# Sums of squares for a retention head: two of four feature tiles added on VectorE, and all weight roundings of the stage on VectorE

## The reference, cut to what matters

```
def retention(xn, w_in, w_out):
    proj = xn @ w_in
    q, k, v, g = split(proj)                 # 1024, 1024, 2048, 2048 columns
    ...
    out = inner + cross                      # per head: decayed (q k^T) v
    out = rms_norm(out).reshape(B, S, H * dv)      # over the 512 features of a head
    return (silu(g) * out) @ w_out

def rms_norm(x):
    return x * rsqrt(mean(x * x, axis=-1) + EPS)
```

## Time and profile before

| | |
|---|---|
| Median of 3 runs | 1396.87 us (1387.72, 1396.87, 1397.72) |
| Profiled execution | 1386.03 us, of which the span from first to last instruction is 1384.2 us |
| TensorE busy, granted clock | 97% of the span, 0.988 |
| VectorE, ScalarE, GpSimd busy | 67%, 50%, 10% |
| Gate slots and heads, output projection | 744 to 802.6 us, 802.6 to 850 us of the span |

### The profile page before, as it was taken

How to read it: one execution, slowest core, us unless ns; L and a number is a source line. 1 busy time by engine, 2 the same in 40 slices (tenths; PEclk the granted TensorE clock), 3 DMA queues, 4 the chain that set the end, 5 groups by cost and what they waited for, 6 DMA issues and landing times.

```text
span 1384.2 us, 24555 instructions
## 1 busy us (share of the span) xinstructions
PE 1342.2 (97%) x9631; PEld 1243.7 (90%) x9631; DVE 924.5 (67%) x1197; ACT 691.9 (50%) x959; POOL 142.6 (10%) x116
## 2 busy tenths in 40 slices
PE   8998999999999999999999999999999979999997
PEld 8997988999988999888999978999888967899986
DVE  6876753677556777447744476877657684799964
ACT  5664344532334544345344565666546374666652
POOL 0000151000000000000000330222200000025410
PEclk9999999999999999999999999999999988999999
DMA  7552322310045555554553354555554521455562
GB/s 278 183 172 84 125 107 92 128 57 31 0 177 184 183 186 182 182 183 164 186 192 133 117 178 172 183 182 182 198 212 153 183 92 57 170 185 182 182 216 103
DMA packets 30314, 213.03 MB, mean 154 GB/s; under 512 B 3488, under 2 KB 3616, under 8 KB 5152
## 3 DMA queue, kind: packets, MB, share of 16 engines
q1 hardware_dynamic: 29088, 206.72, 42.8%
q0 software_dynamic: 1152, 5.24, 1.2%
HBM read 210.90 MB, written 1.05 MB: 153 GB/s over the span
## 4 chain that ended last, share of the span: by engine, by line
PE 88%; DVE 6%; ACT 4%; DMA 1%; issue 1%; SPq 0%; DVEq 0%; ACTq 0%
PE lin L522 54%; PE lin L591 20%; PE aux L2199 2%; PE aux L2213 1%; PE aux L2211 1%; ACT whi L496 1%; PE aux L2343 1%; PE aux L2089 1%; DMA raw<-in_stream 1%; PE aux L2456 1%; PE aux L2359 1%; DVE ht L1288 1%; DVE ro L1809 1%; PE aux L2161 1%; ACT xhi L746 0%
## 5 line engine op out<-in xcount | busy, mean ns | idle before, releaser
L503 DVE TENSOR_TENSOR wlo<-raw,whi 128x2048 fp32r<-128x2048 f32 x182 | 423.2, 2328 | 181.1 <-ACT whi L496 180.7
L522 PE MATMUL lin<-xhi,whi 128*128 128x256 f32 (+1 forms) x1776 | 508.1, 286 | 2.3 <-DVE xlo L1299 1.8
L522 PE MATMUL lin<-xlo,whi 128*128 128x256 f32 (+1 forms) x1776 | 502.7, 283 | 0.0
L522 PE MATMUL lin<-xhi,wlo 128*128 128x256 f32 (+1 forms) x1776 | 500.0, 282 | 0.0
L496 ACT CAST whi<-raw 128x2048 fp32r<-128x2048 f32 x193 | 366.9, 1903 | 216.0 <-DMA raw<-in_stream 183.5
L522 PEld LDWEIGHTS lin<-xhi,whi 128*128 128x128 f32 x1776 | 334.7, 188 | 5.3 <-issue 4.0
L522 PEld LDWEIGHTS lin<-xhi,wlo 128*128 128x128 f32 x1776 | 336.8, 190 | 0.0
L522 PEld LDWEIGHTS lin<-xlo,whi 128*128 128x128 f32 x1776 | 335.4, 189 | 0.4
L689 POOL TENSOR_TENSOR wlo<-raw,whi 128x2048 fp32r<-128x2048 f32 x11 | 51.2, 4652 | 519.0 <-ACT whi L496 335.9
L1897 DVE SCALAR_TENSOR_TENSOR ft<-fy,par,ft 128x254 f32<-128x254 f32 (+1 forms) x176 | 91.0, 557 | 5.9 <-DVE ft L1897 0.2
L591 PE MATMUL lin<-wlo,fhi 128*128 128x512 f32 x176 | 69.6, 396 | 0.0
(11 more groups left out here) (411 smaller groups left out, 2102.7 us busy)
## 6 DMA issues: line engine op xcount, KB each, us to landing
raw<-in_stream SPq DMA_DIRECT2D x193, 1024.0 KB, 4.9
gp<-in_gains POOLq DMA_DIRECT2D x6, 512.0 KB, 3.9
c<-in_const SPq DMA_DIRECT2D x1, 1652.0 KB, 17.5
h<-in_x SPq DMA_DIRECT2D x2, 544.0 KB, 4.0
c<-in_const POOLq DMA_DIRECT2D x1, 1024.0 KB, 5.1
ht<-in_xtok POOLq DMA_DIRECT2D x1, 1024.0 KB, 6.9
out<-ht SPq DMA_DIRECT2D x1, 512.0 KB, 2.6
out<-ht SPq DMA_DIRECT2D x2, 256.0 KB, 2.2
```

Source lines behind the costliest of these rows:

```text
L503: nc.vector.tensor_tensor(wlo[:, s0 % 4], raw[:, s0 % 4], whi[:, s0 % 4].bitcast(F32), ALU.subtract).then_inc(lo_ready, 1)
L522: ins = nc.tensor.matmul(out, a, b, start=start and n == 0, stop=stop and n == 2)
```

## The change

Three edits. (1) A new step `pairs` hh on VectorE stands ahead of `squares` hh in the written order. It adds the second half of the squares (tiles 2 and 3) to the first (tiles 0 and 1), one instruction of 128x512. (2) `squares` waits for that addition and multiplies two tiles by the ones in place of four: eight ones-products in the stage, not sixteen. (3) GpSimd makes no rounding in this stage; VectorE makes the rounding of slot j + 3 behind the eviction of every gate j, and no longer waits for GpSimd ahead of the output projection.

```diff
 RETENTION = [..., ("gate", 3), ("hi", 3), ("silu", 3),
-             ("squares", 0), ("root", 0), ("product", 2), ("readout", 2), ("gate", 4), ("hi", 4), ("finish", 0),
-             ("squares", 1), ("root", 1), ("product", 3), ("readout", 3), ("high", 0), ("gate", 5), ("hi", 5),
-             ("low", 0), ("finish", 1), ("squares", 2), ("silu", 4), ("silu", 5), ("high", 1), ("gate", 6), ("hi", 6),
-             ("low", 1), ("root", 2), ("squares", 3), ("finish", 2), ("gate", 7), ("hi", 7), ("root", 3), ("silu", 6),
+             ("pairs", 0), ("squares", 0), ("root", 0), ("product", 2), ("readout", 2), ("gate", 4), ("hi", 4), ("finish", 0),
+             ("pairs", 1), ("squares", 1), ("root", 1), ("product", 3), ("readout", 3), ("high", 0), ("gate", 5), ("hi", 5),
+             ("low", 0), ("finish", 1), ("pairs", 2), ("squares", 2), ("silu", 4), ("silu", 5), ("high", 1), ("gate", 6), ("hi", 6),
+             ("low", 1), ("root", 2), ("pairs", 3), ("squares", 3), ("finish", 2), ("gate", 7), ("hi", 7), ("root", 3), ("silu", 6),
              ("silu", 7), ("high", 2), ("finish", 3), ("low", 2), ("high", 3), ("low", 3)]
 # GpSimd
-            pool_low(pool, FIRST["rg"] + 6, FIRST["ro"] + 3)
 # VectorE
             def gate(j):
...
-                if j < 3:
-                    load_lo(s + 3, 0)
+                load_lo(s + 3, 0)
+
+            def pairs(hh):
+                after(dve, f"ro{hh}_0")
+                after(dve, f"ro{hh}_1")
+                q = rsq[:, hh % 2]
+                nc.vector.tensor_tensor(q[:, 0:2], q[:, 0:2], q[:, 2:4], ALU.add).then_inc(S("ro_pairs"), 1)
...
-            dve.wait_ge(lo_ready, FIRST["ro"] + 3)
 # TensorE
             def squares(hh):
-                after(pe, f"ro{hh}_0")
-                after(pe, f"ro{hh}_1")
+                pe.wait_ge(S("ro_pairs"), hh + 1)
                 b = fill(f"rn{hh}")
-                for e in range(4):
-                    ins = nc.tensor.matmul(b[:, 0:SEQ], ones[:], rsq[:, hh % 2, e], start=e == 0, stop=e == 3)
+                for e in range(2):
+                    ins = nc.tensor.matmul(b[:, 0:SEQ], ones[:], rsq[:, hh % 2, e], start=e == 0, stop=e == 1)
```

More of the change, by code:

```diff
@@ L1815, in low @@
                     .then_inc(S("rlo"), 1)
-            todo = {"gate": gate, "finish": finish, "low": low}
+            todo = {"gate": gate, "pairs": pairs, "finish": finish, "low": low}
             for name, n in RETENTION:
```

## The result

| | before | after |
|---|---|---|
| Median | 1396.57 us (4 runs, 1387.72 to 1397.72) | 1423.78 us (4 runs, 1409.95 to 1425.06) |
| Ratio | | 1.0224, 95% interval 1.0162 to 1.0285 |
| Profiled execution, span | 1386.03, 1384.2 us | 1425.0, 1423.2 us |
| Granted clock, mean | 0.988 | 0.969 |

A forecast was written before the change was run, and what follows sets the result against it. TensorE was taken to bound the stage, with one 2.46 us hole at its end. Waits of 26.5 us less 3.5 and 2.5, plus 8.0 for the clock, gave 28.5 on 1396.87: 1425 us, range 1405 to 1434.

The forecast's parts named there:

- the turns: TensorE and VectorE wait for each other around the ones-products; net of products and hole, 20.5 us slower.
- the clock: Half-speed stretches after the four waits: 2.4 us for heads 1 to 3, 0.8 for head 0; 8.0 us slower.
- The place at which TensorE waits: Ones-products of heads 0 to 3 wait for additions queued on VectorE behind each gate slot's end; 26.5 us in all.
- What is removed: Half the ones-products (3.46 us) and the stretching of VectorE by GpSimd roundings (hole, 2.46 us): gains of 5.9 us.
- The hole at the third output slot: TensorE's 2.46 us wait at 816.39 in the output projection, for a late low part; forecast to close.
- Rival (a): Additions of heads 0 to 3 are hidden and relief of VectorE counts: 5.9 us faster, 1391; chance 0.08.
- Rival (b): Clock doesn't fall, or one short stretch follows each wait: 20.5 to 27.3 us slower; some 0.25 of the 0.85.
- Rival (c): Clock stays low through the whole stage: 20.5 + 32 us slower, 1449; chance 0.07.
- The level: Runs shown have a median 10.8 us above the profiled execution; the forecast adds 28.5 to the median, 1396.87.

The follow-up runs named there:

- early version: Changed kernel with each addition one place earlier, ahead of the gate slot whose eviction it stood behind; ratio 0.9948 to the kernel before, stage 103.58 us.

## Why the prediction was right

It forecast 1425 us, 28.5 above the median; measured are 1423.78, and 28.7 us in the stage. That the two differ by only 0.2 us is in part luck: the turns were put 0.6 us too high and the clock 0.8 too low. By its own steps:

- **The place at which TensorE waits.** The waits were given as 3.89, 8.14, 9.36 and 5.11 us, 0.17 of each being lost overlap; measured idle times are 3.58, 7.77, 8.90 and 4.72, each 0.14 to 0.3 below the rest. The durations were those of a whole instruction where the next one starts a little earlier (2.20 us from rounding to addition, not 2.28). Moving only the additions, one place after the other, gave 14.3, 6.0 and 2.5 us of waits, and with the place behind the eviction the loss was gone. This is shown.
- **What is removed.** The half of the ones-products, 0.87 us a head in the sum, is gone from TensorE (from gate 3's eviction to gate 4's pass 9.24 us in the early version and 10.10 with the roundings alone), and no step of VectorE is stretched. The hole at the third output slot is closed in the changed kernel. But the closing of the hole is owed to the waits: TensorE is 25 us late, and VectorE has caught up. Without the waits (early version) only 3.0 of the 5.9 us come out, and the roundings alone leave 1.01 us of the hole. Rival (a), 5.9 us faster if the additions were hidden, named the right point of decision and had the wrong price: VectorE becomes the bound of the last quarter of the stage.
- **The clock.** 8.0 us were forecast, 9.4 are counted in the windows, and 8.8 vanish when TensorE is kept at work. The stretches behind heads 1 and 2 lasted 10.2 us, but half of that was the wait itself. The step was sized from the six stretches of the earlier trace rows, and its split (2.4 for each long wait, 0.8 for the short one) was low for the short one: 3.40 busy, 1.7 us lost. Rival (b), at most one short stretch a wait and so at most 6.8 us, covers the measured median too, but the count of 9.4 and the 8.8 are above it. The rule of the Trainium skill ("TensorE: Matmul & The Clock Gate", section "What's actually happening") gave 9.5, nearer than my 8.0: all four waits had the lower level in or behind them.
- **Rival (c)** didn't happen in the stage. But the argument against it, that full clock has always come back within 6.9 us of work, isn't general: at 202.3, where the two kernels do the same work, the clock stayed at 0.50 through 23.90 us of it.
- **The level.** The sum was made on the profiled execution and put on the median. That held, since both kernels' runs lie mostly on the upper level.

## What to carry to other kernels

The price of a small step on a second engine is not its length but everything that stands between the event that frees that engine and the step, in its own queue; here four additions of 0.68 us cost TensorE 25 us of waits, and 2.5 us when they stood in front of the wait for the gate slot instead of behind it. If the input of a step has long been ready and its consumer comes right after an event, put the step ahead of the wait for that event. And count a wait of TensorE of the size of these, 3.5 to 9 us, twice: once as idle time, and once for the half-speed stretch in or behind it, 1.7 to 3.0 us here and 2.3 on average, which did not grow with the wait.

## What the runs showed of the hardware that I had not expected

**Two levels of the whole time.** All but one of the executions of the kernel before lie between 1380 and 1388 or between 1394 and 1399 us, and most of those of the variants are split in the same way. The profiles show one place that fits: in the attention part around 201 us TensorE has waited 2.4 us, and then the clock is at 0.50 either for 3.4 us or, in the changed kernel and in eight variants, for 23.9 us with TensorE busy all the time (the fifth window above). The program is the same there. From the matmul that ends this wait to the one that ends the next wait of over 1 us (199.98 to 234.56 before, 201.64 to 245.21 changed) 34.6 us pass before and 43.6 in the changed kernel: the long stretch makes 9.0 of the 10.7 us by which gate 0 is late. The other 1.7 are already there at 201 us; the changed kernel's trace has one more stretch of 3.4 us, at 120.4. In two variants (the two without additions in which low(2) was moved) the clock didn't fall at 201 us at all, and gate 0 was evicted at 742.84 and 744.57. That profiles on different levels differ by this stretch is shown; what decides between them is open.

**A wait of 2 to 2.6 us may or may not be followed by the lower clock.** There was no such stretch after 2.46 us at 816.39 before, after 2.49 us at 804.88 in the early version and after 2.64 us in the early version with GpSimd's roundings. There was one of 3.4 us after the 2.40 us at 199.98, at the 2.52 us of the additions alone, and after 2.05 us here, in the version with the roundings and low(2) moved:

```profile
819.13 0.78 PE L591 MATMUL lin<-whi,rhi 128*128 128x512 f32 x1 [2.05 <-DVE wlo L503]
```
```profile
819.20:822.60 3.40, 3.40 (x8) 2.73 (x9) 3.40 (x2) 1.15 (x1) 0.00 (x0) 0.50 0.58 243
```

Waits of 1.0 to 1.9 us in this stage had no such stretch behind them, and each of the fourteen from 3.49 to 8.90 us had one in or behind it.

**An addition of 128x512 can take 4.96 us.** In the version with the additions alone it ends, at 782.36, 0.5 us after the GpSimd rounding beside it, as if it had been held until then. The "GPSIMD Engine Reference" of the Trainium skill (section "Specifications") says that GpSimd shares SBUF interfaces with VectorE, in contention with its two-input instructions; the row agrees.
